# An attention and recurrence block on one core: rotary terms by exchanged halves, decay rows by one product, decay masks on VectorE

## What is computed

```python
def hybrid_mixer(h_ctx, h_lat, w_in, conv_w, ...):
    p = (h @ w_in).astype(f32)
    ...
    o_f = gated_delta_rule(q, k, v, g_f, jax.nn.sigmoid(b_f))
    o_b = to_bwd(gated_delta_rule(to_bwd(q), to_bwd(k), to_bwd(v), ...))
    o_gdn = rms_norm(o_f + o_b, gdn_norm_g) * jax.nn.silu(z)
    rq = apply_rope(rq, cos, sin)
    rk = apply_rope(rk, cos, sin) * (HEAD_DIM ** -0.5)
    ...
    o_ret = head_group_norm(r_f + r_b, ret_norm_g) * jax.nn.silu(rg)

def apply_rope(t, cos, sin):
    t1, t2 = t[..., :HALF], t[..., HALF:]
    return jnp.concatenate([t1 * c - t2 * s, t1 * s + t2 * c], axis=-1)

def gated_delta_rule(q, k, v, g, beta):
    G = jnp.cumsum(gc, axis=-1)
    decay = jnp.where(incl, jnp.exp(G[..., :, None] - G[..., None, :]), 0.0)
    A = jnp.where(strict, einsum(kb, kc) * decay, 0.0)
    sol = lax.linalg.triangular_solve(A + I, rhs, lower=True, unit_diagonal=True)
    qk = einsum(qc, kc) * decay
    q_dec = qc * jnp.exp(G)[..., None]
```

## Time and profile before

| quantity | value |
|---|---|
| median of 3 launches | 3382.01 us (3381.61 to 3382.19) |
| profiled execution, device time | 3379.65 us |
| its span | 3377.5 us |
| TensorE busy | 3306.6 us (98%) |
| VectorE, ScalarE, GpSimd busy | 1189.8, 1368.7, 1516.2 us |
| granted TensorE clock, mean | 0.996 of full speed |
| projections | 59.5 to 325.5 us |
| retention and gated delta rule | 325.5 to 539.8 us |

### The profile page before, as it was taken

The page is one execution under the profiler, slowest core; times in us unless marked ns, Lnnn a source line. Parts: engine busy times, 40 slices in busy tenths (PEclk is TensorE's granted clock), DMA queues, the critical chain, the costliest instruction groups (busy, mean ns, idle before and its releaser), DMA issues.

```text
span 3377.5 us, 45592 instructions
## 1 busy us (share of the span) xinstructions
PE 3306.6 (98%) x16746; PEld 2775.3 (82%) x16746; DVE 1189.8 (35%) x1878; ACT 1368.7 (41%) x1976; POOL 1516.2 (45%) x1114
## 2 busy tenths in 40 slices
PE   6999999999999999999999999999999999999998
PEld 4778888888898888888888888888888888888887
DVE  6763775211131115444125111411035452161104
ACT  4444445443244323247225442443333374244423
POOL 2333112554445454545544554455445545445444
PEclk8999999999999999999999999999999999999999
DMA  6332001222222222322222222222222222222222
GB/s 268 129 143 78 1 1 63 100 93 100 94 92 96 99 94 82 106 94 100 94 88 93 94 98 97 79 106 94 99 85 96 100 94 100 94 82 99 97 95 100
DMA packets 90034, 322.22 MB, mean 95 GB/s; under 512 B 9776, under 2 KB 12208, under 8 KB 89776
## 3 DMA queue, kind: packets, MB, share of 16 engines
q1 hardware_dynamic: 88576, 316.71, 26.9%
q10 hardware_dynamic: 1328, 3.67, 0.3%
HBM read 318.24 MB, written 2.10 MB: 95 GB/s over the span
## 4 chain that ended last, share of the span: by engine, by line
issue 40%; POOL 31%; PE 23%; DVE 3%; DMA 1%; POOLq 1%; ACT 1%; SPq 0%; DVEq 0%; ACTq 0%
POOL w_lo L476 31%; PE ps L534 4%; PE ps L535 4%; PE ps L539 4%; DMA ada_first<-ada 1%; PE ps L839 1%; DVE inverse_span L1975 1%; PE ps L1102 1%; PE ps L1097 1%; PE ps L1095 1%; PE ps L554 1%; PE ps L961 1%; PE ps L1121 0%; PE ps L1125 0%; PE ps L1119 0%
## 5 line engine op out<-in xcount | busy, mean ns | idle before, releaser
L476 POOL TENSOR_TENSOR w_lo<-raw,w_hi 128x512 fp32r<-128x512 f32 x1086 | 1484.1, 1389 | 1709.2 <-ACT w_hi L1269 1709.1
L1269 ACT ACTIVATE w_hi<-raw 128x1024 fp32r<-128x1024 f32 x543 | 575.3, 1060 | 1436.9 <-PE ps L539 901.8
L535 PE MATMUL ps<-acts,w_hi 128*128 128x512 f32 x2776 | 1080.0, 389 | 0.0
L534 PE MATMUL ps<-acts,w_hi 128*128 128x512 f32 x2776 | 1079.9, 389 | 0.0
L539 PE MATMUL ps<-acts,w_lo 128*128 128x512 f32 x2776 | 685.6, 389 | 0.0
L539 PEld LDWEIGHTS ps<-acts,w_lo 128*128 128x128 f32 x2776 | 521.1, 188 | 108.1
L534 PEld LDWEIGHTS ps<-acts,w_hi 128*128 128x128 f32 x2776 | 521.2, 188 | 108.0
L535 PEld LDWEIGHTS ps<-acts,w_hi 128*128 128x128 f32 x2776 | 521.1, 188 | 107.9
L2297 DVE TENSOR_TENSOR tmp<-tmp,ps 128x512 f32<-128x512 f32 x110 | 75.6, 687 | 781.8 <-PE ps L539 728.3
L2300 DVE TENSOR_TENSOR acts<-tmp,acts 128x512 f32 x110 | 117.6, 1069 | 154.2 <-ACT acts L1628 154.2
L1095 PE MATMUL ps<-acts,w_hi 128*128 (+1 forms) x440 | 171.2, 389 | 0.0
(11 more groups left out here) (385 smaller groups left out, 3966.2 us busy)
## 6 DMA issues: line engine op xcount, KB each, us to landing
raw<-stream SPq DMA_DIRECT2D x543, 512.0 KB, 3.2
ada_behind<-ada SPq DMA_DIRECT2D x32, 512.0 KB, 3.4
ada_first<-ada SPq DMA_DIRECT2D x8, 1024.0 KB, 12.6
X<-x_in ACTq DMA_DIRECT2D x1, 2048.0 KB, 8.5
...
```

The lines of the kernel that those rows point to most:

```text
L476: last = nc.gpsimd.tensor_tensor(w_lo[:, slot, part, :], raw[:, slot % RAW, part, :], f32(w_hi[:, slot, part, :]), ALU.subtract)
L534: mm(o, w_hi[:, s, k, :], xh, start=start, stop=False, skip_group_check=True)
L535: mm(o, w_hi[:, s, k, :], xl, start=False, stop=False, skip_group_check=True)
L1269: A(w_hi[:, s, :, :], raw[:, s % RAW, :, :], ACT.Copy).then_inc(s_hi, 1)
```

## The change

Four things are changed.

1. **Rotary terms.** The products by the rotation matrix are gone. ScalarE copies a projection of rk or rq out of PSUM twice, once straight and once with its halves exchanged (two copies of 64 partitions each); the sign is in the sine table. All three VectorE operations of the rotary term stand directly one after another. The product by ones for item 0 moves from behind item 2 to behind item 3.
2. **Decay rows.** Once, two products put the cumulated gates of all chunks and heads in rows (`gate_cols`); after that `decay_rows` is one fp32r product of 512 columns for each direction (`chosen` by `head_rows`) in place of four float32 products.
3. **Who does what.** The triangle and the decayed queries go from GpSimd to VectorE (`masked_queries`, `decayed_queries`), the squares of the means from ScalarE to GpSimd. GpSimd has nothing else to do in the steps.
4. **Places.** Extra work of a level is cut in halves, one between the level's two products (`under_copies`) and one behind the second (`under_merges`); tables say at which level. Queries by state stand among the last products. Some buffers have new addresses, `units` comes earlier, the squares of the retention norm stand at the ends of steps 0 and 1, and the waits for `s_go` ahead of `opening` stand only before the two banks that need them.

```diff
+ROWS_AT, KEYS_AT, STATE_AT = (1, 1, 3, 3, 3, 0), (3, 4, 5, 5, 5, 0), (0, 2, 3, 3, 3, 1)
+ABOVE_AT, BELOW_AT, BOTH_AT = (3, 5, 5, 5, 5, 0), (5, 5, 6, 6, 6, 0), (5, 6, 6, 6, 6, 0)
...
-            for s in range(NCC, NC):
-                for d in range(2):
-                    pool.wait_ge(s_na[d], s + 1)
-                    nc.gpsimd.tensor_tensor(gt[d][0][:, :, :], gt[d][0][:, :, :],
-                                            cst1[:, d, :].unsqueeze(1).to_broadcast([P, H, P]), ALU.mult).then_inc(s_em, 1)
-                for d in range(2):
-                    c, qd = order[d][s], gts[s % 2][d][6]
-                    pool.wait_ge(s_eg[d], s - NCC + 1)
-                    nc.gpsimd.tensor_tensor(qd[:, :, :], qd[:, :, :], qT[:, :, c * P - CTX:(c + 1) * P - CTX],
-                                            ALU.mult).then_inc(s_qd, 1)
...
+                for j in () if i < 3 else (0, 1) if i == 3 else (i - 2,):
+                    kind, h = items[j]
+                    if kind in NORMED:
+                        pe.wait_ge(s_squares, n_aux[j])
                         if n_aux[j] >= 2:
                             pe.wait_ge(s_aux_read, n_aux[j] - 1)
...
+                        for d in range(2):
+                            mm(ps[7][:, 256:256 + P], gate_cols[d][:, :], cst1[:, d, :], start=(d == 0), stop=(d == 1))
...
                     if s > NCC:
                         pe.wait_ge(s_qe, 2 * (s - NCC) + d - 1)
-                    for h in range(H):
-                        col = 24 * d + 4 * order[d][s] + h
-                        last = mm(ps[4 * d + 3][:, h * P:(h + 1) * P], tok[:, 0, col:col + 1].to_broadcast([P, P]),
-                for d in range(2):
-                    c = order[d][s]
+                    elif s:
+                        pe.wait_ge(s_na[d], s)
+                        pe.wait_ge(s_gS[d], s - 1)
+                    row = NC * d + order[d][s]
+                    mm(ps[4 * d + 3][:, :], chosen[:, row:row + 1].to_broadcast([P, P]), head_rows[:, :],
+                       start=True, stop=True).then_inc(s_rows, 1)
...
+            def under_copies(s, lev):
+                if s >= NCC and lev in (1, 2) and s < NC - 1:
+                    keys_queries(s, lev - 1, 0)
+                if s == NC - 1 and lev > 2:
+                    keys_queries(s, (lev - 3) // 2, (lev - 3) % 2)
+                if s and lev - STATE_AT[s] in (0, 1):
+                    keys_state(s, lev - STATE_AT[s], 0)
+                if s < NC - 1:
+                    if lev == ROWS_AT[s] and s < NCC:
+                        decay_rows(s + 1)
+                    if lev == KEYS_AT[s]:
+                        key_products(s + 1, 0, 0)
+                        key_products(s + 1, 0, 1)
+                    if lev == KEYS_AT[s] + 1:
+                        key_products(s + 1, 1, 1)
+                if s == 0 and lev in (2, 4):
+                    ret_sums(lev - 2)
+            def under_merges(s, lev):
+                if s >= NCC and lev in (1, 2) and s < NC - 1:
+                    keys_queries(s, lev - 1, 1)
+                if s and lev - STATE_AT[s] in (0, 1):
+                    keys_state(s, lev - STATE_AT[s], 1)
+                if s < NC - 1 and lev == KEYS_AT[s]:
+                    key_products(s + 1, 1, 0)
+                if lev == ROWS_AT[s] and s >= NCC:
+                    decay_rows(s + 1)
+                if s >= NCC and lev == 6:
+                    state_queries(s, 0)
...
                 key_values(s, 0)
                 key_values(s, 1)
+                if s:
+                    pe.wait_ge(s_rv, NC)
+                    query_keys(NCC)
                 turn(2 * NC + 2 * s)
                 turn(2 * NC + 2 * s + 1)
-            pe.wait_ge(s_rv, NC)
-            query_keys(NCC)
...
+                    if s >= NCC and d == 0:
+                        state_queries(s, 1)
+                if s < 2:
+                    ret_squares(2 * s)
...
                             pe.wait_ge(s_hi, n_hi.up())
+                            if second and banks[j] in (2, 6):
+                                pe.wait_ge(s_go[banks[j] // 4], 4)
                         high_high(j, k)
...
-            pe.wait_ge(s_go[0], 4)
-            pe.wait_ge(s_go[1], 4)
             opening(FIRST_OUT[:4], s_yh, s_y, n_y, second=delta_squares)
...
+                        c, half = cbuf(i), (slice(0, P // 2), slice(P // 2, P))
+                        parts = [(slice(0, CTX), C[:, 0:CTX]), (slice(CTX, TOK), L)] if kind == "rk" else [(slice(0, LAT), L)]
+                        for cols, bank in parts:
+                            A(b[:, cols], bank[:, :], ACT.Copy)
+                            for a in range(2):
+                                last = A(c[half[a], cols], bank[half[1 - a], :], ACT.Copy)
+                        last.then_inc(s_pread, 1)
...
-                        TT(dst[:, h, :], b[:, 0:m], rope_sb[:, o:o + m], ALU.mult).then_inc(s_cdone, 1)
+                        TT(c[:, 0:m], c[:, 0:m], rope_sb[:, o + m:o + 2 * m], ALU.mult)
+                        link(TT(dst[:, h, :], b[:, 0:m], rope_sb[:, o:o + m], ALU.mult))
+                        dve.sem_inc(s_cdone, 1)
+                        TT(dst[:, h, :], dst[:, h, :], c[:, 0:m], ALU.add).then_inc(s_roped, 1)
...
+            def masked_queries(s, d):
+                t = gts[s % 2][d]
+                link(TT(t[0][:, :, :], t[0][:, :, :], cst1[:, d, :].unsqueeze(1).to_broadcast([P, H, P]), ALU.mult))
+                dve.wait_ge(s_qk, 2 * (s - NCC) + d + 1)
+                TT(t[5][:, :, :], bank(4 * d + 3), t[0][:, :, :], ALU.mult).then_inc(s_qe, 1)
+
+            def decayed_queries(s, d):
+                c, qd = order[d][s], gts[s % 2][d][6]
+                dve.wait_ge(s_eg[d], s - NCC + 1)
+                TT(qd[:, :, :], qd[:, :, :], qT[:, :, c * P - CTX:(c + 1) * P - CTX], ALU.mult).then_inc(s_qd, 1)
...
                 if s == NCC + 1:
                     for d in range(2):
                         dve.wait_ge(s_rkz[d], NC - 1)
+                    units()
             for d in range(2):
                 negative_matrix(0, d)
             both_matrices(0)
             pairs(0)
...
-                    if lev == 5 and s < NC - 1:
-                        negative_matrix(s + 1, 0)
...
-                    if s >= NCC and lev == 1:
-                        for d, c, b, t in both:
-                            dve.wait_ge(s_em, 2 * (s - NCC) + d + 1)
-                            dve.wait_ge(s_qk, 2 * (s - NCC) + d + 1)
-                            TT(t[5][:, :, :], bank(b + 3), t[0][:, :, :], ALU.mult).then_inc(s_qe, 1)
-                    if s and lev == 2:
-                        for d in range(2):
-                            right_side(s, d)
+                    if s in (1, 2) and lev == 1:
+                        ret_variances(2 * (s - 1))
+                    if NCC <= s < NC - 1 and lev in (1, 2):
+                        masked_queries(s, lev - 1)
+                    if s == NC - 1 and lev in (4, 6):
+                        masked_queries(s, lev // 2 - 2)
+                    if s and lev - STATE_AT[s] in (1, 2):
+                        right_side(s, lev - STATE_AT[s] - 1)
                     if s == 0 and lev in (2, 4):
                         ret_means(lev - 2)
-                    if s == 1 and lev == 1:
-                        ret_centred()
-                    if s == 1 and lev in (4, 5):
-                        ret_variances(2 * (lev - 4))
-                    if s == NC - 1 and lev == 4:
+                    if s in (NCC, NCC + 1) and lev == 3:
+                        ret_centred(2 * (s - NCC))
+                    if s >= NCC and lev in (4, 5):
+                        decayed_queries(s, lev - 4)
+                    if s == NC - 1 and lev == 5:
                         head_result(0)
-                    if s == NC - 1 and lev == 5:
-                        head_result(1)
-                        head_low(0)
-                    if s < NC - 1 and lev == 5:
-                        negative_matrix(s + 1, 1)
-                        both_matrices(s + 1)
-                if s < NC - 1:
-                    units()
+                    if s < NC - 1:
+                        if lev == ABOVE_AT[s]:
+                            negative_matrix(s + 1, 0)
+                        if lev == BELOW_AT[s]:
+                            negative_matrix(s + 1, 1)
+                        if lev == 6:
+                            units()
+                        if lev == BOTH_AT[s]:
+                            both_matrices(s + 1)
                 if s < NC - 1:
                     pairs(s + 1)
                     turned_blocks(s + 1, 1)
                 if s == NC - 1:
-                    head_result(2)
-                    head_low(1)
-                    head_result(3)
+                    head_low(0)
+                    head_result(1)
```

312 lines of the change are left out of this document (150 added, 162 removed).

## The result

The changed kernel takes 3354.16 us (median of 4 launches, 3353.69 to 3355.4) against 3382.1 us (4 launches, 3381.61 to 3383.94): ratio 0.9917, 95% interval 0.99 to 0.9934, so 27.9 us less. Taken again in five launches it was 3354.89 us beside 3382.57, the same ratio. The forecast was 3358, with a range of 3351 to 3369: right in direction and range, and some 4 us too timid. Its profiled execution took 3355.4 us (span 3353.4).

The account below looks back on a forecast made before the run. TensorE was taken as the bound, full in the projections, with stalls from rounds with VectorE in the steps. Terms −6.4 − 2.5 − 13.6 − 1.4 = −23.9 gave 3355.7 us, a median of 3358, range 3351 to 3369.

Parts of the forecast that it names:

- Rotary terms: Projections: removed rotation products save 9.0 us, gate rows add 0.5, a wait at `arow` 2.1; net −6.4, between −8.5 and −4.
- Up to the first level: Ahead of step 0's first level: `query_keys` earlier −0.5, first decay rows −1.33, `units` ahead of a wait −0.7; together −2.5.
- The steps: Steps 0 to 5: fewer decay-row records, halved extra work and a relieved select give −13.6, bounds −7 and −20.
- Step 1: Second step: −1.3 for decay rows and −3.8 of stalls from the norm's chain, together −5.1 (−2.5 to −6).
- Tail: `opening` of w_out: only two banks wait for VectorE's last output sums, some 0.5 of 1.86 us left; −1.4 (0 to −1.9).
- Rival B: VectorE becomes the bound of steps 2 to 4, which then gain nothing (7.0 us less); 3365 us; chance 0.17.
- Rival C: More than forecast: no wait at `arow` (2.1), steps within 1 us of TensorE's records; 3347 to 3351 us; chance 0.08.
- Rivals D and E: D: projections give their saving back, 3364 us, chance 0.07. E: slower, merges wait for extra work, above 3388.8, chance 0.03.

Follow-up runs that it names:

- the three runs on the projections: Edits of the changed kernel: `arow` copies ahead of the reciprocal, 3352.54 us; item 0's product behind item 2, 3353.06; early copies plus early `mod`, 3351.6.

## Why the prediction was right, and what it mis-sized

**Rotary terms: right.** The added wait is 1.83 (forecast 2.1, 0 to 4.5), the net −6.3 in an undisturbed execution against −6.4; that leaves 8.1 us for the products removed less those added, forecast at 8.5. No run puts the rotation products back, so this part rests on the two traces and the count. What the forecast lacked is the clock: it said that nothing is to be lost by it, because the clock was 1.00 before. The change made a pause that was not there before, and behind it the clock fell in 4 of the 9 traces that have the wait, and at this place in none of the 4 that don't. Retention began at 320.8 to 321.1 us in the four and at 319.4 to 319.8 in the other five, so the price is about 1.4 us.

**Up to the first level: right**, −2.5 and −2.5. TensorE's wait ahead of the first level is 1.73 us where it was 2.37, −0.6 for a forecast of −0.7.

**The steps: the mechanism right, the term too small.** Forecast −12.6 for steps 0 to 4, measured −18.9 (−0.3 − 7.3 − 2.9 − 4.2 − 4.2). In step 3 the forecast had 13.6 us for the four levels between the first and the fifth merge and 14.6 behind them (126 records and 0.5 of stalls); they last 12.58 and 14.19, where they lasted 14.92 and 16.01 before. So 1.0 of the missing 1.4 us is in the levels, set at 3.5, 3.2, 3.3 and 3.6 us by rounding gaps up; they last 3.32, 2.91, 3.06 and 3.29. The other 0.4 are stalls behind the fifth merge that are gone.

The runs give each part's price when it alone is undone in steps 3 and 4: decay rows 1.1, halves 2.2, GpSimd's products 2.2, less 0.4 for VectorE's own four. That sums to 5.1 against 4.2 measured, so these are prices within the changed kernel and don't add up to the gain. The largest difference is in GpSimd's. The forecast put its relief at 1.4 us, and that is what the kernel before shows: 1.12 on the select and 0.30 on the two copies. But there VectorE waited for TensorE behind them, and the only wait of TensorE for VectorE in the same stretch is one of 0.38 us, for the copy behind the select. So most of the 1.4 us seems to have been hidden. In the changed kernel the same products would block both copies, the select and the pairs, 2.2 us, and nothing hides it. How much of the gain from the kernel before is GpSimd's alone was not measured. The Trainium skill ("SBUF — State Buffer", section "SBUF: two separate sides") has an exclusive lock between GpSimd and VectorE with two SBUF inputs or in its two-port mode; the trace agrees for the select (0.74 against 1.70) and for the copies (0.76 for two against 1.83).

**Step 1: size off.** The forecast took 219 records as 24.5 us. Eight of them are records of 512 columns for the norm's squares, and these are longer. Four of them in order of time, in the changed kernel:

```profile
375.22 1.88 PE L868 MATMUL ps<-tmp,ones 128*128 128x512 f32 x4
376.94 1.95 PE L940 MATMUL ps<-gt,gt 128*128 128x128 f32 x16
```

That is 1.72 us for four, 0.43 each and not 0.112, so TensorE's work there was 27.1 and the stalls 5.3, not 7.9. By the traces the step lost 4.9 us of TensorE's work (squares 1.72 to step 0, decay rows 1.79, 12 records of keys by queries to step 2) and 2.4 of stalls; moving the centring back there costs 1.55 us.

**Tail: the sum right, its reason wrong.** −2.4 came, and the wait of 1.86 us in `opening` shrank to about the forecast 0.5. It is 0.41 now:

```profile
511.51 2.78 PE L993 MATMUL ps<-acts,w_hi 128*128 128x512 f32 x11 [0.41 <-DVE ogdn L1970]
```

But the moved waits, which were to give this 1.4 us, are worth 0.14, so the right size was luck. Before, VectorE came to both output sums only at 538.44, behind norm work. In the changed kernel it adds each direction's as its product ends:

```profile
510.68 0.69 DVE L1970 TENSOR_TENSOR ogdn<-ogdn,ps 128x512 f32<-128x512 f32 x1 [0.81 <-PE ps L945]
```

It was idle for 0.81 us ahead of the last one, so little is left to wait for, wherever the waits stand. That the order of VectorE's work made this is read from the two traces; no run changed it by itself.

**The total: right, and nearer than its parts.** The touched part gave 28.5 to 29.1 us against 23.9. Against the kernel before's own execution the stretch behind it took 4.4 back, for which the forecast had nothing. The medians, with 27.9 us, are the fairer measure, and against them the forecast's 24 is 4 us short, nearly all of it in the steps.

**Rival B** (VectorE becomes the bound) came half true: VectorE does set the first levels, but it sets them at less than before, since TensorE's extra work no longer stands in the round. In steps 3 and 4 TensorE is as full (26.5 of 26.7). The sign that the forecast named for B or E, VectorE's idle time before merges gone while TensorE's before the second products grows, came by its first half only. The passage of the Trainium skill that the forecast set against the edit ("Perfetto Trace Analysis", section "Optimizing Scalar/DVE Operations") itself adds that moving operations between GpSimd and VectorE "might not help"; here moving them to GpSimd made steps 2 to 4 longer by 1.35 to 1.82 us. **Rival C** was the nearest by the steps, though not by the wait at `arow`. **Rivals D and E** did not come: the three runs on the projections show one wait of 1.4 us or none, and in the levels of step 3 the merges wait 0.2 us in all; taking the halves away costs 2.2 us a step.
